# Dense feed-forward of a decoder trunk in six units instead of seven, with two modulation chunks summed in two of its steps

## The reference, cut to what matters

```python
D_FF = 2816
D_FF_EXPERT = 3584

def swiglu(h, wg, wu, wd):
    return (jax.nn.silu(h @ wg) * (h @ wu)) @ wd
...
"ada_w": nrm((DEPTH, D, 6 * D), 0.5 * D ** -0.5),
"ffn_wg": nrm((N_DENSE, D, D_FF), D ** -0.5),
"ffn_wu": nrm((N_DENSE, D, D_FF), D ** -0.5),
"ffn_wd": nrm((N_DENSE, D_FF, D), D_FF ** -0.5),
```

## Time and profile before

| | |
|---|---|
| median of 3 runs | 1533.02 us (1532.82 to 1533.63) |
| profiled execution, its own time | 1533.67 us |
| its span | 1531.9 us |
| TensorE busy | 1435.1 us, 94% |
| VectorE busy | 470.6 us, 31% |
| ScalarE busy | 197.6 us, 13% |
| DMA traffic | 481.64 MB, mean 314 GB/s |

### The profile page before, as it was taken

How to read it: one execution, slowest core, us unless ns; L and a number is a source line. 1 busy time by engine, 2 the same in 40 slices (tenths; PEclk the granted TensorE clock), 3 DMA queues, 4 the chain that set the end, 5 groups by cost and what they waited for, 6 DMA issues and landing times.

```text
span 1531.9 us, 17250 instructions
## 1 busy us (share of the span) xinstructions
PE 1435.1 (94%) x6928; PEld 700.8 (46%) x6928; DVE 470.6 (31%) x945; ACT 197.6 (13%) x427; POOL 3.4 (0%) x32
## 2 busy tenths in 40 slices
PE   6899899999999999989877899989999999999997
PEld 2475765555554666653222333424234434334432
DVE  4478735434433465343100011100101221101011
ACT  1123223000003132320000000000000000000000
POOL 0000000000000000000000000000000000000000
PEclk9999889999999999989999999999999999999999
DMA  9945535896776332149999999999999999999996
GB/s 343 361 160 196 178 121 179 262 338 242 264 276 242 111 111 111 56 157 396 415 412 401 414 412 412 416 412 415 409 411 399 412 412 415 410 414 411 409 394 269
DMA packets 161506, 481.64 MB, mean 314 GB/s; under 512 B 18536, under 2 KB 36328, under 8 KB 147088
## 3 DMA queue, kind: packets, MB, share of 16 engines
q1 hardware_dynamic: 159976, 478.65, 81.0%
q10 hardware_dynamic: 1448, 1.84, 0.4%
HBM read 479.41 MB, written 1.06 MB: 314 GB/s over the span
## 4 chain that ended last, share of the span: by engine, by line
PE 74%; DMA 16%; DVE 5%; SPq 2%; ACT 2%; issue 1%; DVEq 0%; ACTq 0%
PE bank L1670 24%; PE bank L1703 12%; PE bank L1544 10%; DMA ring<-in_moe_wu 7%; PE bank L1266 6%; PE bank L1562 5%; DMA ring<-in_moe_wd 4%; PE bank L1508 3%; DMA ring<-in_moe_wg 3%; PE bank L1255 2%; DMA ring<-in_ada_w 1%; SPq L837 1%; PE bank L1609 1%; DVE ada_acc L1808 1%; PE bank L1686 1%
## 5 line engine op out<-in xcount | busy, mean ns | idle before, releaser
L1670 PE MATMUL bank<-ring,h_T 128*32 128x512 f32 (+1 forms) x2240 | 299.4, 594 | 32.8 <-DMA ring<-in_moe_wu 24.9
L1703 PE MATMUL bank<-ring,m_qk_T 128*32 128x512 f32 (+2 forms) x1344 | 247.1, 594 | 18.0 <-DMA ring<-in_moe_wd 17.3
L1670 PE MATMUL bank<-ring,cmp_region 128*128 128x512 f32 x448 | 196.4, 593 | 0.0
L1670 PEld LDWEIGHTS bank<-ring,h_T 128*32 128x32 f32 (+1 forms) x2240 | 90.6, 115 | 225.9 <-issue 224.1
L1703 PEld LDWEIGHTS bank<-ring,m_qk_T 128*32 128x32 f32 (+2 forms) x1344 | 88.0, 127 | 172.6 <-issue 171.4
L1544 PE MATMUL bank<-ring,h_T 128*128 128x384 f32 (+1 forms) x448 | 156.8, 503 | 0.7 <-DVE m_s_region L2203 0.7
L1670 PEld LDWEIGHTS bank<-ring,cmp_region 128*128 128x128 f32 x448 | 83.9, 190 | 100.7 <-issue 100.7
L1266 PE MATMUL bank<-ring,h_T 128*128 128x512 f32 (+1 forms) x320 | 116.1, 512 | 0.8 <-ACT wide L955 0.5
L1544 PEld LDWEIGHTS bank<-ring,h_T 128*128 128x128 f32 x448 | 83.3, 190 | 61.3 <-issue 15.5
L1101 ACT ACTIVATE m_qk_T<-bank 128x512 f32<-128x512 f32 x35 | 20.9, 597 | 630.7 <-PE bank L1686 630.1
L2402 DVE SCALAR_TENSOR_TENSOR m_s_region<-m_s_region,bank 128x512 f32<-128x512 f32 x35 | 24.1, 688 | 243.0 <-PE bank L1670 243.0
(11 more groups left out here) (353 smaller groups left out, 1004.8 us busy)
## 6 DMA issues: line engine op xcount, KB each, us to landing
ring<-in_moe_wg SPq DMA_DIRECT2D x112, 1024.0 KB, 20.8
ring<-in_moe_wu SPq DMA_DIRECT2D x112, 1024.0 KB, 18.4
ring<-in_moe_wd SPq DMA_DIRECT2D x112, 1024.0 KB, 19.9
ring<-in_ada_w SPq DMA_DIRECT2D x28, 1024.0 KB, 8.8
ring<-in_ada_w SPq DMA_DIRECT2D x10, 2048.0 KB, 14.1
ring<-in_w_in SPq DMA_DIRECT2D x10, 2048.0 KB, 10.9
ring<-in_ffn_wg SPq DMA_DIRECT2D x6, 1536.0 KB, 9.7
ring<-in_ffn_wu SPq DMA_DIRECT2D x6, 1536.0 KB, 9.0
```

Source lines behind the costliest of these rows:

```text
L1670: last = mm(b[c0:c1, :], xT[st.team % 2][:, k, c0:c1], w, start=k == 0, stop=k == KC - 1)
L1703: last = mm(ps[half][c0:c1, :], hbT[:, unit, 128 * f + c0:128 * f + c1], w[:, D * (f % 2) + 512 * half:D * (f % 2) + 512 * half + 512], st ...
```

## The change

Five units of 512 features and one of 256 take the place of six of 384 and one of 512, so there are 12 steps. The 14 chunks are divided over 12 steps (`SUMMED_IN`): chunks 0 and 1 are summed in step 0, chunk n in step n-1 for n from 2 to 7, chunks 7 and 8 both in step 6, and chunk n in step n-2 for n from 9 to 13. In a step VectorE sums that step's chunks and then takes those of the step before; TensorE reduces the chunks of step j-1 in `after(j)`. The second chunk of a step is loaded one ring load behind the first.

```diff
-FF_UNITS = tuple((384 * u, 384 if u < 6 else 512) for u in range(7))
+FF_UNITS = tuple((512 * u, 512 if u < 5 else 256) for u in range(6))
...
-SEQ += [(0, "ffn", c) for c in range(21)]
+SEQ += [(0, "ffn", c) for c in range(3 * len(FF_UNITS))]
...
-ADA_AFTER = {AT[(0, "ffn", 0)] + 3 * (n // 2) + (5 if n % 2 else 3): n for n in range(len(ADA_FFN))}
+SUMMED_IN = [n - (n >= 1) - (n >= 8) for n in range(len(ADA_FFN))]
+SUMS_OF = [[n for n, s in enumerate(SUMMED_IN) if s == j] for j in range(2 * len(FF_UNITS))]
+ADA_AFTER = {AT[(0, "ffn", 0)] + 3 * (s // 2) + (5 if s % 2 else 3) + SUMS_OF[s].index(n): n for n, s in enumerate(SUMMED_IN)}
...
-    return [Step(w, tt, 2 * tt, [AT[(0, "ffn", 3 * u + p)] for p in range(3)], None, tt == 0, tt == TT - 1, u == 0, u == 6)
+    return [Step(w, tt, 2 * tt, [AT[(0, "ffn", 3 * u + p)] for p in range(3)], None, tt == 0, tt == TT - 1, u == 0, u == len(FF_UNITS) - 1)
...
-            swiglu(ffn, dense_steps(), 0, after=lambda j: ada_reduce(*ADA_FFN[j - 1]) if 1 <= j < 13 else None)
+            def reduce_summed(j):
+
+                for n in SUMS_OF[j - 1] if j else ():
+                    if n < 12:
+                        ada_reduce(*ADA_FFN[n])
+
+            swiglu(ffn, dense_steps(), 0, after=reduce_summed)
...
-            def modulation(j):
+            def modulation(step):
+
+                for n in SUMS_OF[step]:
+                    sum_chunk(n)
+                for n in SUMS_OF[step - 1] if step else ():
+                    if n < 12:
+                        ada_take(*ADA_FFN[n])
+                    if n in (5, 11):
+                        mod_scale(1, n // 6)
+
+            def sum_chunk(j):
...
-                if 1 <= j < 13:
-                    ada_take(*ADA_FFN[j - 1])
-                if j in (6, 12):
-                    mod_scale(1, j // 12)
```

More of the change, by code:

```diff
@@ L275 @@
 ADA_FFN = [(0, 10), (0, 11)] + [(1, c) for c in range(12)]
-SEQ += [(0, "ffn", c) for c in range(21)]
+SEQ += [(0, "ffn", c) for c in range(3 * len(FF_UNITS))]
 SEQ += [(1,) + k for k in WINS + WOUT]
 AT = {k: n for n, k in enumerate(SEQ)}
-ADA_AFTER = {AT[(0, "ffn", 0)] + 3 * (n // 2) + (5 if n % 2 else 3): n for n in range(len(ADA_FFN))}
+SUMMED_IN = [n - (n >= 1) - (n >= 8) for n in range(len(ADA_FFN))]
+SUMS_OF = [[n for n, s in enumerate(SUMMED_IN) if s == j] for j in range(2 * len(FF_UNITS))]
+ADA_AFTER = {AT[(0, "ffn", 0)] + 3 * (s // 2) + (5 if s % 2 else 3) + SUMS_OF[s].index(n): n for n, s in enumerate(SUMMED_IN)}
+assert len(ADA_AFTER) == len(ADA_FFN) and SUMMED_IN[-1] == len(SUMS_OF) - 1
 PRE = RING - 1
```

## The result

The changed kernel takes 1567.22 us (median of 6 runs, 1564.29 to 1573.21); the kernel before took 1532.8 us in the same comparison (6 runs). The ratio is 1.0235 with a 95% interval of 1.0219 to 1.0251: 34 to 38 us slower. The forecast was 1559.8 us with a range of 1548 to 1567. In the comparisons behind this one, a single execution of the kernel before (3832 us) and one of `e7_all_mended` (2144 us) stand far outside all others and are left out of the ratios.

What follows compares the result with a forecast made beforehand. TensorE was taken to bound the dense stage, with delays passing through one to one. Terms -0.5 + 14.4 + 6.0 + 6.9 = +26.8 us on 1533.67, less 0.65 for the median, gave 1559.8 us; range 1548 to 1567.

Steps and rivals of the forecast that it cites:

- Loads and the rest: Ring loads: same bytes in 2 MB loads, delayed ring loads hidden by two steps (some 40 us); cost 0.
- From there to the end, the same length as before: Sign for the profile after: from the second mixer's transposes to the end, no change in length.
- The double steps: Dense stage, two sums in steps 0 and 6: TensorE waits 7.2 us each for a take behind a sum; +14.4 us.
- The clock: Behind three TensorE stops of some 7 us: clock falls to its lower level, 2.0 us lost each; +6.0 us.
- The last unit: End of dense stage: TensorE stands 7.0 us before the second mixer's transposes, behind chunk 13's sum and tile 0's residual; +6.9 us.
- Wider units: Dense stage: up products give back 0.2 us and three waits at the ends move; -0.5 us in all.
- More of both: Rival: clock loss 3.4 us each, last unit 8, stalls 16; +33.7 us, 1567 us; chance 0.08.
- a chain not seen: Remainder of 0.02 for an unforeseen chain, anywhere in the kernel: half laid on no change, half on faster.

Runs made afterwards that it cites:

- e7_all_mended: The changed kernel with the edits of e1, e3, e4 and e9 together; 1537.67 us, ratio 1.0028 to the kernel before.
- e1: The changed kernel with the expert loads' ring slots put in order of release (4, 5, 0, 1, 2, 6, 3); 1561.34 us, ratio 1.0185.
- e2: The kernel before with the expert loads' slots in the order 4, 5, 0, 1, 2, 6, 3; 1535.53 us, ratio 1.0021.
- e10: The kernel before with the expert loads' slots in the order 0, 5, 1, 2, 3, 4, 6, the last-released slot first; 1540.53 us, ratio 1.0061.
- e3: The changed kernel, but behind a double step VectorE takes the first chunk ahead of its sum; 1545.71 us, ratio 1.0079.
- e6: The changed kernel's sums and chunk loads with the old units (six of 384, one of 512, 14 steps); 1556.36 us, ratio 1.0152.
- e5: The changed kernel with seven unread products of 512 columns on TensorE in each of two stalls; 1562.57 us, ratio 1.0199.
- e4: The changed kernel with VectorE adding the residual of tile 0 ahead of the sum of chunk 13; 1559.89 us, ratio 1.0191.
- e9: The changed kernel with chunk 13 loaded one ring load earlier; 1563.81 us, ratio 1.0224.
- e8: The kernel before with the expert loads' slots in the order 1, 2, 3, 4, 6, 5, 0; 1532.24 us, ratio 1.0004.

## Why the prediction was wrong

**The failed step: "Loads and the rest".** It put the loads at 0, what hides them being the two steps that a unit is loaded ahead, and its list of signs says "From there to the end, the same length as before". The loads of the dense stage's weights do cost nothing: between 286 and 500 us TensorE waits for no load in the trace after. But I looked at how late each of them would be and never at where the loads behind them come to lie. Three loads fewer turned the ring by three slots. The expert loads then first waited for a slot that is released late, and +4.1 us of wait and +1.7 us of clock in front of the experts were missing from the sum. e1 took 5.9 us away with this alone, e2 and e10 brought a wait into the kernel before with nothing else changed. With these 5.8 us the sum is 32.6, for 32.9 in the spans and 34.4 between the medians. That it comes so near is in part luck: the dense stage took 1.1 us more than predicted, and three other stretches came out 0.8 us shorter with no cause known. The measured median lies only 0.2 us above the range, and the profiled execution (1566.58 us) inside it; what was wrong is the missing term.

**The double steps: right.** Predicted 7.2 us each at the take behind the sum; measured 7.27 and 7.19, released by that take. e3 reduces them to 0.94, and e6 shows that they belong to the sums and not to the units.

**The clock: right mechanism, size too small.** Predicted 6.0 for three stops. From the start of the second reduction to the turn it took 9.66 us, where the same two (395.94 to 403.67 in the trace after) take 7.73: 1.9 us; behind the second stall 10.50 for 7.76 (450.72 to 458.48): 2.7; from the transposes of tile 0 to those of tile 1 10.87, for 8.29 before: 2.6. Together 7.2 us. The lines for the undisturbed cases:

```profile
395.94 1.02 PE L1219 MATMUL bank<-ada_acc,const 128*128 128x512 f32 x2
...
403.67 0.60 PE L1554 MATMUL bank<-const,m_s_region 128*128 128x128 f32 x4
...
450.72 0.95 PE L1222 MATMUL bank<-const,ada_acc 128*128 128x1 f32 x8
...
458.48 0.60 PE L1554 MATMUL bank<-const,m_s_region 128*128 128x128 f32 x4
```

e5 shows the first two apart from the stalls. The Trainium skill (page "TensorE: Matmul & The Clock Gate", section "Why this matters for your kernels") advises against idle gaps between bursts of matmuls. This case agrees: stops of 7 us each cost 1.9 to 2.7 us more than their length, and filling two of them with useless work was faster than stopping.

**The last unit: right.** Predicted 7.0 us of idle time where 0.15 was; measured 6.94. The wait for chunk 13's data was 2.59 us for 2.7 predicted (its halves landed 10.1 and 12.2 us after issue, for 10.3 and 12.0 taken from the earlier trace rows). e4 and e9 take off both parts one by one.

**Wider units: right as far as can be told.** What the stops and the clock leave of the 27.9 us is 27.9 - 14.5 - 6.8 - 7.2 = -0.6 us, for -0.5. This is a remainder with the errors of the others in it; no run measures the wider units alone.

**The rivals.** "More of both" came closest in its time, 1567 us, but not for its reasons: the clock lost 7.2 and not 10.2 us, the two stalls 14.5 and not 16, the last unit 6.8 and not 8. No rival spoke of the slots; the 0.02 kept for a chain not seen was laid on the wrong side. The upper end of the range, 1567, was the sum of the known terms at their bounds and had no room for an unknown cost.

## What to carry to other kernels

A change in the length of a list of loads can move every later load to another slot of the ring: follow the list to its end, and see which slot the next stage asks for first and who releases it. Before two items are put in one step, write down what each engine waits for in program order: here a take that was always early stood behind a sum that could only start when the other engine had finished. A stop of TensorE can cost more than its length: here those of 7 us did, by the clock behind them, and those of 0.94 us did not. And when a unit becomes shorter on one engine, look at what the other engine did meanwhile: here a last step half as long no longer covered VectorE's sum.

## What the runs showed of the hardware

The same program doesn't always lose its clock at the same places. The runs of the kernel before with a mean granted clock of 0.990 and 0.991 took 1528.55 to 1531.62 us, those with 0.985 and 0.986 took 1531.64 to 1536.08 us. In the profiles the dense stage starts at 239.69 us in one execution of the kernel before and at 234.66 us in e8, which differs only in later loads; between 120 and 180 us the granted clock is 0.91 in the one and 1.00 in the other. The second mixer, from the gate projection to the gather, took 183.16 us before, 182.84 after, and 187.4 in both e1 and e3, although neither changes what TensorE does in it; its gate projection alone took 3.62 us in two of these and 5.31 us in the other two. A single profile may so be 5 us off in a stage that a change doesn't touch; this is why each loss here was read from the products next to the stop.

What a stop costs in clock doesn't grow with its length in these runs. The first expert product takes 13.87 us at full clock. Behind a wait of 3.34 us (e2) it took just that; behind 3.54 (e5), 3.95 (e4), 4.05 (after) and 4.08 us (e9) it took 15.57, behind 3.94 (e3) 16.29, and behind 11.16 us (e10) 15.77.
